# A diffusion step on one core: a convolution matrix built after the chunk matmuls, a shorter routing chain, and first modulation rows loaded by two engines

## What is computed

```python
mod = silu(c) @ w_mod + b_mod                    # 6 rows of 1024, for c_ctx and for c
h = rmsnorm(x) * norm1_w * (1 + scale1) + shift1
z = h @ w_in                                     # 512 | 512 | 512 columns
u_ssm = z[:, :512]; u_g, v_g = split(gelu(z[:, 512:]))
# mixer A: 32 groups of 16 channels, a 64-wide complex diagonal state each, both directions
s[l] = abar * s[l-1] + bbar @ u_ssm[l];  y = Re(C s_fwd) + Re(C s_bwd) + D * u_ssm
y = gelu(y); y = y * sigmoid(y @ w_glu)
y_g = u_g * (w_s @ layernorm(v_g) + b_s)         # mixer B
x = x + gate1 * (concat(y, y_g) @ w_out)
h2 = rmsnorm(x) * norm2_w * (1 + scale2) + shift2
# 16 SwiGLU experts, top 2 inside the best of 4 groups, weights normalised
x = x + gate2 * moe(h2);  out = rmsnorm(x) * final_norm_w
```

## Time and profile before

| | us |
|---|---|
| device time, median of 3 runs | 656.39 |
| lowest and highest of them | 653.26 and 656.78 |
| the profiled execution | 653.9 |
| its span in the trace | 652.0 |
| PE busy | 519.8 (80%) |
| DVE busy | 227.2 (35%) |
| ACT busy | 147.0 (23%) |

### The profile page before, as it was taken

How to read it: one execution, slowest core, us unless ns; L and a number is a source line. 1 busy time by engine, 2 the same in 40 slices (tenths; PEclk the granted TensorE clock), 3 DMA queues, 4 the chain that set the end, 5 groups by cost and what they waited for, 6 DMA issues and landing times.

```text
span 652.0 us, 7377 instructions
## 1 busy us (share of the span) xinstructions
PE 519.8 (80%) x2541; PEld 263.7 (40%) x2542; DVE 227.2 (35%) x627; ACT 147.0 (23%) x282; POOL 74.6 (11%) x168
## 2 busy tenths in 40 slices
PE   2799998999979379985256999999997888889810
PEld 0346898754439344445242333333332222223200
DVE  2587918599994210173321011110100000001017
ACT  3537926301112541021021001010100000001023
POOL 2000000488500100500310000000000000000030
PEclk9889659999999769995568999999997888879965
...
GB/s 267 349 327 0 130 113 18 208 151 34 382 387 134 263 407 333 0 65 0 120 267 385 101 395 347 201 250 386 426 421 425 424 422 423 425 422 345 34 188 117
DMA packets 41135, 164.51 MB, mean 252 GB/s; under 512 B 2776, under 2 KB 3576, under 8 KB 36368
## 3 DMA queue, kind: packets, MB, share of 16 engines
...
...
## 4 chain that ended last, share of the span: by engine, by line
issue 47%; PE 34%; DMA 6%; DVE 6%; ACT 4%; SPq 2%; POOL 1%; POOLq 0%; DVEq 0%
PE psum L559 6%; DMA arena<-in_w_mod 5%; PE psum L402 4%; PE psum L465 3%; PE psum L507 3%; PE psum L457 2%; PE psum L491 2%; PE psum L532 2%; PE psum L552 2%; ACT arena L847 2%; PE psum L471 2%; PE psum L472 2%; PE psum L586 1%; SPq L303 1%; DVE arena L1113 1%
## 5 line engine op out<-in xcount | busy, mean ns | idle before, releaser
L629 PE MATMUL psum<-arena 128*64 128x512 f32 x672 | 164.1, 645 | 29.6 <-DMA arena<-in_w_up 19.6
L629 PEld LDWEIGHTS psum<-arena 128*64 128x64 f32 x672 | 52.3, 148 | 127.6 <-issue 108.8
L642 PE MATMUL psum<-arena 128*64 128x512 f32 x336 | 77.5, 603 | 2.3 <-ACTq L909 2.3
L1286 DVE TENSOR_TENSOR arena<-arena,psum 128x256 f32<-128x256 f32 x21 | 8.8, 421 | 188.8 <-ACT arena L893 188.8
L402 PE MATMUL psum<-arena 128*2 128x256 f32 x384 | 48.1, 408 | 10.9 <-DMA arena<-in_w_mod 10.9
L642 PEld LDWEIGHTS psum<-arena 128*64 128x64 f32 x336 | 25.9, 139 | 49.7 <-issue 49.7
L559 PE MATMUL psum<-arena 128*128 128x512 f32 x96 | 41.4, 592 | 0.0
...
L893 ACT ACTIVATE arena<-psum 128x256 f32<-128x256 f32 x21 | 8.0, 383 | 140.4 <-PE psum L629 116.9
L402 PEld LDWEIGHTS psum<-arena 128*2 128x2 f32 x384 | 18.1, 90 | 38.0 <-issue 13.5
L898 ACT ACTIVATE arena<-psum 128x512 f32<-128x512 f32 x21 | 12.5, 597 | 68.4 <-PE psum L642 68.4
L559 PEld LDWEIGHTS psum<-arena 128*128 128x128 f32 x96 | 18.2, 190 | 22.8 <-issue 22.5
...
## 6 DMA issues: line engine op xcount, KB each, us to landing
...
arena<-in_w_down SPq DMA_DIRECT2D x16, 2048.0 KB, 21.8
arena<-in_w_mod SPq DMA_DIRECT2D x12, 2048.0 KB, 12.7
...
```

The lines of the kernel that those rows point to most:

```text
L629: last = mm(bank[0][HALF * t:HALF * t + HALF, :], xs[:, k, :], gu[:, :, k, t * 256:t * 256 + 256], start=(k == 0), stop=(k == KD - 1))
L642: last = mm(bank[4][HALF * h:HALF * h + HALF, :], hiddenT[:, s * P + t * HALF:s * P + t * HALF + HALF], dn[:, 2 * t + s, h * 512:h * 512 + ...
```

## The change

What it does, part by part:

1. `units[0..3]` become row pairs (`mod_rows`): both column groups for two of the eight blocks of 128 rows, 8 KB runs. SP loads pairs 1 and 3, ACT pairs 0 and 2, ahead of X. PE multiplies each pair for all 2048 columns (`first_modulation`); ACT and DVE share the copy of the result. The A parameters now stand first on ACT's queue, the states (`srow`) go by POOL, log_dt by SP. PE transposes the B parameters ahead of the modulation, and waits for the vectors (`vec_in`) between pair 1 and pair 2.
2. DVE makes the four real B tables before the modulation columns, the imaginary ones after, then all of C. DVE's wait for `root_done` stays where it was, ahead of the copy of B.
3. BB is transposed right after part 0, copied by ACT and DVE in turn; V is copied by both in turn.
4. The convolution matrix is made after V: 144 matmuls with 32-wide weights, in groups of four that write to four different quarters of the partitions; POOL prepares `Cbd`, `Bbd` and the direct term `diagD`; ACT gathers L in 16 copies (`kernel_row`), 8 of them after the first GELU.
5. `modulation(13)` and `(14)` move behind the output projection, between the router's matmuls and before the counts. Expert 1 is therefore loaded after that.
6. gT moves over the modulation rows; ACT's GELUs wait for those rows being in memory, not for `spatial_ready`.
7. h2 of the first tokens is transposed ahead of the last half of the output projection; the counts are two matmuls in place of nine; DVE's chain from counts to row numbers is 11 operations, and the weights `wts` are computed behind it.
8. Only the first 128 sorted rows are transposed before the first gate and up pass, the other five groups after it.

```diff
+        def mod_rows(i):
+            return ("mod", i, w_mod[:, 2 * i:2 * i + 2, 0:2 * D])
...
-        units = [mod_half(0, 0), mod_half(0, 1), mod_half(1, 0), mod_half(1, 1), in_part(0), in_part(1), in_part(2)] \
+        units = [mod_rows(0), mod_rows(1), mod_rows(2), mod_rows(3), in_part(0), in_part(1), in_part(2)] \
             + [mod_half(m, h) for m in (2, 4, 3, 5) for h in range(2)]
...
             def prologue_unit(i):
-                sp.dma_start(view(slot(place[i]), KD, 512), units[i][2]).then_inc(unit_sem(i)[0], 16)
-
-            for i, name in enumerate(("state_ssm_re", "state_ssm_im")):
-                sp.dma_start(arow[64 + 32 * i:96 + 32 * i, :],
-                             io[name][0, 0].rearrange("d (g t) n -> (d g) (t n)", t=2)).then_inc(S("a_in"), 16)
-            prologue_unit(0)
+                n = 2 if i < 4 else KD
+                sp.dma_start(view(slot(place[i]), n, UNIT // n), units[i][2]).then_inc(unit_sem(i)[0], 16)
+
+            for i in range(2):
+                sp.dma_start(dtr[32 * i:32 * i + 32, 0:2],
+                             io["ssm_log_dt"][0].rearrange("d (g t) -> (d g) t", t=2)).then_inc(S("dt_in"), 16)
             for i, name in enumerate(("ssm_b_re", "ssm_b_im")):
                 sp.dma_start(rawB[32 * i:32 * i + 32, :],
...
-            prologue_unit(2)
             prologue_unit(3)
...
+            sp.wait_ge(S("diag_done"), 1)
...
-            sp.wait_ge(S("bt_ready"), 16)
+            sp.wait_ge(S("lk_ready"), 1)
...
-            sp.wait_ge(S("spatial_ready"), 3)
+            sp.wait_ge(S("yt_done"), 4)
...
+            def first_modulation(i):
+
+                pe.wait_ge(*unit_sem(i))
+                w = view(slot(place[i]), 2, 2 * D)
+                for kk in range(2):
+                    k = 2 * i + kk
+                    for c in range(2):
+                        for t in range(2):
+                            last = mm(bank[(4, 7)[c]][32 * t:32 * t + 2, :], sil[:, k, :],
+                                      w[:, kk, t * D + c * 512:t * D + c * 512 + 512],
+                                      start=(k == 0), stop=(k == KD - 1))
+                last.then_inc(S("unit_used"), 1)
+
...
+            tr(bank[5][:, 0:96], vrows[0:96, :], ident[0:96, 0:96])
+            tr(bank[5][:, 96:160], srow[0:64, :], ident[0:64, 0:64]).then_inc(S("vec_ready"), 1)
+            first_modulation(2)
+            first_modulation(3)
             pe.wait_ge(S("xn_done"), 3)
-            pe.wait_ge(S("mrow_done"), 3)
+            pe.wait_ge(S("vec_copied"), 2)
             x_columns(0)
-            pe.wait_ge(S("vec_copied"), 1)
-            x_columns(1)
-            pe.wait_ge(S("mrow_done"), 4)
...
             for i in range(16):
                 last = tr(bank[6][:, 2 * i:2 * i + 2], mrow1[0:2, i * P:(i + 1) * P], ident[0:2, 0:2])
             last.then_inc(S("mod_a_ready"), 1)
+            x_columns(1)
 
...
-            pe.wait_ge(S("bb_done"), 1)
-            for q in range(Q):
-                out = bank[6 + q // 16][:, (q % 16) * 32:(q % 16) * 32 + 32]
-                mm(out, BB[0][:, q, :], Cbd[:, 0, q, :], start=True, stop=False)
-                last = mm(out, BB[1][:, q, :], Cbd[:, 1, q, :], start=False, stop=True)
-            last.then_inc(S("lk_ready"), 1)
+            pe.wait_ge(S("put"), 8)
+            for n in range(16):
+                if n >= 4:
+                    pe.wait_ge(S("bt_copied_a") if n % 2 == 0 else S("bt_copied_v"), n // 2 - 1)
...
+            pe.wait_ge(S("put"), 16)
+            pe.wait_ge(S("diag_done"), 1)
+
+            def drive_in(ri, q):
+                return Bbd[:, q, :] if ri == 0 else BB[1][:, q, (96, 0)[q // GP]:(128, 32)[q // GP]]
+
+            for s in range(4):
+                def kernel_out(g, lo, hi):
+                    return bank[6 + s // 2][32 * g:32 * g + 32, (s % 2) * 224 + lo:(s % 2) * 224 + hi]
+
+                for d in range(2):
+                    lo, hi, t = ((128, 224, 0), (0, 96, 32))[d]
+                    for ri in range(2):
+                        for g in range(4):
+                            q = d * GP + 4 * s + g
+                            mm(kernel_out(g, lo, hi), drive_in(ri, q), CA[:, ri, q, t:t + 96],
+                               start=(ri == 0), stop=(ri == 1))
+                for d in range(2):
+                    for ri in range(2):
+                        for g in range(4):
+                            q = d * GP + 4 * s + g
+                            mm(kernel_out(g, 96, 128), drive_in(ri, q), Cbd[:, ri, q, :],
+                               start=(d == 0 and ri == 0), stop=False)
+                for g in range(4):
+                    last = mm(kernel_out(g, 96, 128), ident[0:32, 0:32], diagD[0:32, 4 * s + g, :],
+                              start=False, stop=True)
+            last.then_inc(S("lk_ready"), 1)
...
+            for i in range(7, 13):
...
+            for n in range(6):
+                t, h = divmod(n, 2)
+                if n == 5:
+                    h2_columns(0, 2)
+                out_part(t, h, 0).then_inc(S("wo_ready"), 1)
             pe.wait_ge(S("rw_in"), 32)
+            pe.wait_ge(S("x1_done"), 4)
+            h2_columns(1, 4)
             route(0)
+            modulation(13, 6, True).then_inc(S("mrow_ready"), 1)
             route(1)
-            h2_columns(2)
+            h2_columns(2, 2)
             route(2).then_inc(S("logits_ready"), 1)
+            pe.wait_ge(S("mrow_done"), 7)
+            modulation(14, 6, True).then_inc(S("mrow_ready"), 1)
...
+            mm(bank[3][:, 0:NT * NE], tri[:, :], mk.rearrange("p t e -> p (t e)"), start=True, stop=True)
+            mm(bank[3][:, NT * NE:2 * NT * NE], ones[:, :], mk.rearrange("p t e -> p (t e)"), start=True,
+               stop=True).then_inc(S("ranks_ready"), 1)
...
+            sorted_columns(0)
...
+            for t in range(1, 6):
+                sorted_columns(t)
...
+            for i in (0, 2):
+                act.dma_start(view(slot(place[i]), 2, 2 * D), units[i][2]).then_inc(unit_sem(i)[0], 16)
...
                 if k >= 2:
-                    put_b(k - 2)
+                    put(k + 2)
                 act.wait_ge(S("xt_ready"), k + 1)
...
+                b, t = divmod(n // 2, CH)
+                last = A(chunk_dst(t, b), chunk_src(t, b), ACT.Copy)
+                if n == 14:
+                    last.then_inc(S("u_done_a"), 1)
+                act.wait_ge(S("bt_ready"), n + 1)
+                ri, q = divmod(4 * n, Q)
+                A(Bt[:, ri, q:q + 4, :], bank[4 + n % 4][:, :].rearrange("p (a b) -> p a b", a=4),
+                  ACT.Copy).then_inc(S("bt_copied_a"), 1)
...
+            def kernel_row(ti):
+
+                for g in range(4):
+                    last = A(L.rearrange("p (b h x) c -> p b h x c", b=2, h=2)[32 * ti:32 * ti + 32, :, :, g, :],
+                             psum[32 * g:32 * g + 32, 6:8, 0:448].rearrange("p b (h c) -> p b h c", h=2)[
+                                 :, :, :, 96 - 32 * ti:224 - 32 * ti], ACT.Copy)
+                return last
+
+            act.wait_ge(S("lk_ready"), 1)
+            kernel_row(0)
+            kernel_row(1)
...
+                if c == 0:
+                    kernel_row(2)
+                    kernel_row(3).then_inc(S("l_gathered"), 1)
...
-            act.wait_ge(S("spatial_ready"), 3)
+            for m in (2, 4, 3):
+                act.wait_ge(S(f"modd_in{m}"), 16)
...
+            square(0)
+            square(1)
+            h2_copy(0)
+            h2_copy(1)
+            square(2)
+            h2_copy(2)
+            h2_copy(3)
+            row_half(6)
+            h2_copy(4)
...
+            def drive(o, t):
+                i = 4 * o + t
+                x, y, op = ((0, 1, ALU.subtract), (1, 0, ALU.add))[o]
+                if i > 0:
+                    dve.wait_ge(S("made"), i)
+                d(tt(prod1, Bb[:, x], over_h(pwB[:, 0, t, :]), ALU.mult))
+                v(tt(prod2, Bb[:, y], over_h(pwB[:, 1, t, :]), ALU.mult))
+                make(i, prod1, prod2, op)
 
...
+                drive(0, t)
+            dve.wait_ge(S("ct_raw_ready"), 1)
+            raw_copy(CT, 2)
+            dve.wait_ge(S("vec_ready"), 1)
+            cp(vecT[:, 0:96], bank[5][:, 0:96]).then_inc(S("vec_copied"), 1)
+            cp(s0c.rearrange("p a b -> p (a b)"), bank[5][:, 96:160]).then_inc(S("vec_copied"), 1)
+            dve.wait_ge(S("unit_used"), 4)
+            for t in range(2):
+                last = cp(mrow1[:, t * D + 512:t * D + D], bank[7][32 * t:32 * t + 2, :])
+            last.then_inc(S("mod_a_rows"), 1)
+            dve.wait_ge(S("vec_copied"), 2)
+            dve.wait_ge(S("mod_a_ready"), 1)
+            v(tt(modT, bank[6][:, 0:32].rearrange("p (m k s) -> p m s k", m=2, s=2),
+                 vecT[:, 32:48].rearrange("p (m k) -> p m k", m=2).unsqueeze(2).broadcast_to([P, 2, 2, KD]),
+                 ALU.add))
...
+            for n in range(1, 16, 2):
```

(40 more changed lines are left out.)

391 lines of the change are left out of this document (167 added, 224 removed).

## The result

| | before | after |
|---|---|---|
| device time, median of 4 runs each on one chip (us) | 655.18 | 637.08 |
| lowest and highest | 653.26, 656.78 | 636.12, 639.00 |
| span of the profiled execution | 652.0 | 635.2 |
| mean granted clock of TensorE | 0.876 | 0.907 |

A forecast was written before the change was run, and what follows sets the result against it. No single engine was taken to bound the kernel. From 653.9 us, terms +14.1 - 25.3 + 20 - 10.9 - 15.9 - 8.5 + 1.5 = -25.0 gave 628.9 us; 8-in-10 range 617 to 645, own range 622 to 635.

The forecast's parts named there:

- the trap: At the start, DVE's wait for the root of X precedes B's copy and all tables; part 0 starts +14.1 us later.
- the bound of 42: Upper bound in us for X's arrival, if units 4 and 5 get in front; 33 was taken, lower bound 29.
- DVE's tables bind: Between part 0 and V, DVE's table operations decide: 25.3 of the 35.5 us; the stretch changes by -25.3.
- the bias row: Bias matmuls at 0.11 us each, giving 15.8 us for the new matrix's 144; basis of the 18 us taken.
- The light start: Rival: X in at 29 us, matrix 13 us, no half clock behind it: 618 us; chance 0.15.
- this cover: Between V and y, DVE's scan hides beside PE's 86 us of work with 12 us to spare.
- The GELUs: From y through the GLU: GELUs overlap y's banks, -12.9, and GLU runs at full clock, -3.0; together -15.9 us.
- Routing: From output projection's end to the scatter: -4.6 us up to the mask, -4.9 from there, +1.0 inside the projection; -8.5.
- The scatter: At entry to the experts, expert 1's 6.3 MB leave about with the scatter: 0 to 4 us, +1.5 taken.
- Tiles without overlap: Rival: the new matrix's matmuls cost 0.227 us each as V's do, 32.7 us instead of 18: 643.6 us; chance 0.17.
- X late: Rival at the start: X in at 42 us because later SP loads get in front: 638 us; chance 0.15.
- The slower case: Rival: new matrix without overlap at half clock, 0.40 us each, 57.6 us: 668.5 us, slower than before; chance 0.03.

The follow-up runs named there:

- e5: Changed kernel with all four modulation row pairs back on SP's queue, ACT's queue carrying X and the vectors alone: 621.1 us, ratio 0.950.
- e1: Changed kernel with X and the vectors ahead of the two modulation pairs on ACT's queue: 628.1 us, ratio 0.960.
- e7: Changed kernel with three of ACT's six table scalings moved in between the h1 columns: 637.3 us, ratio 0.974.
- e9: Changed kernel with ACT's table scalings spread between columns and GpSimd's preparation held back until DVE's last table is made: 634.4 us, ratio 0.970.
- e4: Changed kernel with the 144 small matmuls of the convolution matrix done twice over, result unchanged: 648.9 us, ratio 0.992.
- e6: Changed kernel with ACT's 16 GELUs of y made to wait until the spatial product is done: 653.9 us, ratio 0.999.
- e11: Changed kernel with pairs on SP's queue, reciprocal behind first table, scalings spread, GpSimd held back, expert 1's loads behind sorted rows' loads: 602.2 us, ratio 0.920.
- e8: Changed kernel with modulation unit 13 moved from the router back ahead of y, beside the scan: 640.4 us, ratio 0.978.
- e3: Changed kernel with expert 1's loads issued behind the loads of the sorted rows instead of ahead: 628.2 us, ratio 0.961.

## Why the prediction was right, and where it was not

**Right by sum, wrong in its largest terms.** 8.2 us are missing from the forecast. The terms that were off are +5.6 (start), +2.8 (part 0 to V), +1.6 (V), -11.9 (end of V to y), -0.2 (y to the GLU's end and projection), +3.0 (routing), +9.4 (scatter), and -2.1 (first experts). That is 22.4 too little and 14.2 too much, and it is luck that so much of it cancels. "y near 194" came true at 193.5 in the same way, by one error against another; the terms up to there add up to 195.4.

**The start: mechanism right, X too early.** The order of DVE's list was the trap, and it shows as foretold: an idle stretch of 23.4 us ahead of the reciprocal. From X's arrival to part 0 the working gave 25.8 us (33 to 58.8), and it was 26.1 (38.33 to 64.38). All the rest of the miss is X: it was in at 38.3, not 33. The working had the bound of 42 for the case that units 4 and 5 get in front of X, and left them out of the 33. They did get in, in part. SP sent them off at 26.75 and 30.2 us, and by 38.3 us the queues had moved (q1 has SP's loads, q10 ACT's; packets, MB, share):

```profile
26.75 3.80 SPq L302 DMA_DIRECT2D arena<-in_w_in  x2
...
DMA packets 2985, 12.70 MB, mean 331 GB/s; under 512 B 511, under 2 KB 686, under 8 KB 1832
...
q1 hardware_dynamic: 1594, 6.80, 51.9%
q10 hardware_dynamic: 1198, 5.84, 42.3%
```

SP had 5.2 MB in front, so 1.6 MB of units 4 and 5 went by ahead of X's end. At the 400 GB/s moved from 26.75 to 38.3 us they took 3.9 us; without them X would have been in near 34 (an estimate; no run held these units back). The step that failed is thus the count of the bytes: 12.7 MB, not 11.0. That the plain quotient of 11.0 MB at 307 GB/s, with the 3 us ahead of it, gives 39 is one error against another, since the queues ran faster, at 331.

The Trainium skill ("DMA: Bandwidth & Descriptors", on issuing engines) held in that the second queue brought no bandwidth: the first 32 us moved 319 GB/s against 307, and 325 in e5 with all pairs on SP's queue. What the working never asked is when the first pair would reach PE: e5 against e1, both with X first, shows that pairs on two queues cost 7 us: what one queue delivers in turn two deliver together, late. The Trainium skill's same page ("Queues, rings and completion order") has each DMA engine take turns between queues packet by packet; that fits pairs landing at 18.0 and 28.9 us in place of 9.8 onward.

**Part 0 to V: 35.5 said, 38.3 measured.** "DVE's tables bind" holds (e7), but not at 0.69 each to the end. The working placed POOL's preparation about where it ran ("near 9 us"; it ran from 85.1 to 95.2) and only asked whether it would be done in time, not what it does to DVE beside it: 2.2 us on the last tables. With ACT's scalings spread and POOL held back, e9 gives 2.1 of the 2.8 back. ACT's six scalings behind the last column end 1.4 us after DVE's last table (93.15 and 91.74), so they were nearly as late; spreading them alone gave 0.8. POOL held back alone wasn't tried.

**V: 14.5 said, 16.1 measured.** It is the same work. Behind an idle 1.78 us it began at full clock, and from 104 to 107 us the granted clock was 0.50. In e4, e6, e9 and e11 V stayed at full clock and took 14.50; in e8 it took 17.76. The edits of e4, e6 and e8 stand behind V, so they aren't the reason, and what decides it wasn't found.

**The new matrix: 18 said, 6.5 measured.** This is the largest wrong term; even the lowest bound of the working, 7.9, was above it. I held to the bias row (0.11 us each) and refused the half of it. 144 products took 0.045 us each with a gap of 1.17 in them, at full clock, so the half clock that was added wasn't there either, nor behind it: z started at once at its usual pace. The Trainium skill ("TensorEngine Tiling (Array Packing)", "Instruction Overhead") gave an estimate of 7.2 us, or twice that with the weight loads. The trace lies below even the smaller: 5.3 us without the gap, and the 32 matmuls of L531 begin within 0.41 us, 13 ns each, where the Trainium skill's 60 cycles are 25. The weight loads cost nothing of their own, with 6.03 us of them beside 6.83 of PE in the window at 118. The light start, which was to lead to 618, had a matrix of 13: the matrix came out lighter still, but its X at 29 us did not come.

**The cover that would be gone.** "If the matrix took only 6 us, this cover would be gone" is what happened: PE is done with its list at 191.4 and waits 2.12 us; DVE's scan runs from 120.36 to 193.4, as long as before. Its first and last operation in the changed kernel:

```profile
120.36 0.38 DVE L1211 TENSOR_TENSOR arena<-arena 128x64 f32<-128x64 f32 x1 [0.50 <-DVE arena L1205]
...
193.11 0.28 DVE L1216 TENSOR_TENSOR arena<-arena 128x64 f32<-128x64 f32 x1
```

PE's row at 193.49 names no releaser; the wait for the scan's states stands ahead of it, and the scan ends 0.1 us before. The working had 12 us to spare there; the matrix and z's half clock came 13.5 cheaper, and what goes beyond is lost in the wait. e4 confirms the slack, and so does e8.

**The GELUs: right to 0.1 us**, overlap and clock, and e6 shows what hangs on it.

**Routing: 3.0 too good.** From mask to scatter it was 3.4, as said. The working put unit 13 at 3.9 at full clock, and it took 5.8 with its bias, since the clock had dropped between short steps (0.72 from 271 to 277); the third set of router matmuls took another 0.9 more than said. Unit 14, at 6.6, is under DVE's chain. In e3 and e9 unit 13 ran at full clock in 4.0, and projection to scatter took 23.1 against the 22.6 of the working, so 2.5 of the 3.0 are the clock of this execution. Unit 13 in the changed kernel:

```profile
271.17 5.31 PE L416 MATMUL psum<-arena 128*2 128x256 f32 x32
```

**The scatter: 1.5 said, 10.9 measured.** The working saw that expert 1's 6.3 MB leave with the scatter and gave that 0 to 4 us, from no row. It never put the scatter's own bytes beside them. The queues between 289 and 316 us of the changed kernel (packets, MB, share of the 16 engines):

```profile
q1 hardware_dynamic: 816, 6.29, 60.8%
q0 software_dynamic: 864, 3.15, 28.5%
```

Together 9.4 MB, at the 391 GB/s of the window 24 us; the weights left at 289.35, and the loads of the sorted rows at 315.31. The sum was there to be made: the two queues finish together, as the pairs did at the start, and the scatter, for which everything waits, with them. e3 shows cause and cure.

**Rivals.** Tiles without overlap (643.6) are excluded by the matrix's price. X late was half true, 38 and not 42, and for the reason given: later loads of SP got in front, with 1.6 MB instead of 4.2. The slower case never came near.
